# The order of the three partial products in a split-precision matmul group

## What is computed

```
def swiglu(x, w_gate, w_up, w_down):
    return (jax.nn.silu(x @ w_gate) * (x @ w_up)) @ w_down

h = h + 0.5 * swiglu(rmsnorm(h, ffn1_norm[l]), ffn1_w_gate[l], ffn1_w_up[l], ffn1_w_down[l])
proj = rmsnorm(h, mix_norm[l]) @ w_in[l]
```

## Time and profile before

| | |
|---|---|
| median of 3 runs | 2159.9 us (2159.9 to 2159.99) |
| the profiled execution, its time | 2160.47 us |
| the profiled execution, its span | 2158.5 us |
| mean granted TensorE clock | 1.0 |
| PE busy | 2152.0 us, 15592 matmuls |
| PEld busy | 2035.5 us, 15592 loads |
| DVE, ACT, POOL busy | 1560.7, 1221.6, 470.3 us |
| HBM read | 389.65 MB |

### The profile page before, as it was taken

One profiled execution on the slowest core, in us unless ns is written; L12 is line 12 of the kernel. 1 busy time (PEld: TensorE's weight loads), 2 busy tenths in 40 slices (PEclk: granted clock), 3 DMA queues, 4 the chain that ended last, 5 costly groups with the idle time before them and its releaser, 6 DMA issues.

```text
span 2158.5 us, 38713 instructions
## 1 busy us (share of the span) xinstructions
PE 2152.0 (100%) x15592; PEld 2035.5 (94%) x15592; DVE 1560.7 (72%) x2591; ACT 1221.6 (57%) x2047; POOL 470.3 (22%) x514
## 2 busy tenths in 40 slices
PE   9999999999999999999999999999999999999999
PEld 9999999999999999988988999889888999999888
DVE  8755977665765587876697586975876688887863
ACT  6544466444544456665566444654655677676652
POOL 1000532420340052231053000430321011101420
PEclk9999999999999999999999999999999999999999
DMA  8655435975785543565466554755565766664653
GB/s 279 222 162 183 144 118 159 237 185 177 193 209 182 171 157 111 183 209 187 160 207 205 189 186 144 233 189 191 187 195 176 210 200 172 178 195 142 227 177 104
DMA packets 424225, 395.81 MB, mean 183 GB/s; under 512 B 16864, under 2 KB 420448, under 8 KB 424048
## 3 DMA queue, kind: packets, MB, share of 16 engines
q1 hardware_dynamic: 410336, 375.22, 55.7%
q0 software_dynamic: 13424, 17.78, 4.0%
q10 hardware_dynamic: 288, 0.34, 0.0%
HBM read 389.65 MB, written 7.41 MB: 184 GB/s over the span
## 4 chain that ended last, share of the span: by engine, by line
PE 98%; DVE 1%; ACT 1%; DMA 0%; issue 0%; SPq 0%; ACTq 0%
PE ps L1755 30%; PE ps L1751 25%; PE ps L1753 17%; PE ps L1754 17%; PE ps L2097 1%; PE ps L2095 1%; PE ps L2096 1%; PE ps L1770 1%; PE ps L2063 0%; PE ps L2047 0%; PE ps L1873 0%; PE ps L2076 0%; PE ps L1918 0%; DVE t L1234 0%; PE ps L2030 0%; PE ps L2031 0%
## 5 line engine op out<-in xcount | busy, mean ns | idle before, releaser
L1755 PE MATMUL ps<-t 128*128 128x256 f32 (+1 forms) x5456 | 1547.4, 284 | 0.0
L1755 PEld LDWEIGHTS ps<-t 128*128 128x128 f32 x5456 | 1028.4, 188 | 0.1
L1234 DVE TENSOR_TENSOR t<-t 128x1024 fp32r<-128x1024 f32 (+1 forms) x722 | 875.7, 1230 | 162.2 <-ACT t L882 161.6
L1753 PE MATMUL ps<-t 128*128 128x272 f32 (+1 forms) x3036 | 875.7, 288 | 0.4 <-DVE t L1465 0.3
L1754 PE MATMUL ps<-t 128*128 128x272 f32 (+1 forms) x3036 | 865.3, 285 | 0.0
L882 ACT ACTIVATE t<-t 128x1024 fp32r<-128x1024 f32 (+1 forms) x722 | 728.3, 1030 | 229.2 <-PE ps L1755 223.6
L1751 PE MATMUL ps<-t 128*128 128x512 f32 x2420 | 840.2, 390 | 0.0
L1753 PEld LDWEIGHTS ps<-t 128*128 128x128 f32 x3036 | 570.8, 188 | 6.0 <-issue 3.3
L1754 PEld LDWEIGHTS ps<-t 128*128 128x128 f32 x3036 | 573.7, 189 | 0.9
L1751 PEld LDWEIGHTS ps<-t 128*128 128x128 f32 x2420 | 454.1, 188 | 95.0
L806 POOL TENSOR_TENSOR t<-t 128x256 f32<-128x256 f32 x110 | 100.6, 915 | 694.1 <-ACT t L1000 694.1
(11 more groups left out here) (208 smaller groups left out, 1583.8 us busy)
## 6 DMA issues: line engine op xcount, KB each, us to landing
t<-ffn_w_in SPq DMA_DIRECT2D x88, 1024.0 KB, 5.2
t<-ffn_w_gate SPq DMA_DIRECT2D x42, 1024.0 KB, 5.4
t<-ffn_w_up SPq DMA_DIRECT2D x42, 1024.0 KB, 7.4
t<-attn_w_qkv SPq DMA_DIRECT2D x72, 512.0 KB, 5.5
t<-ffn_w_down SPq DMA_DIRECT2D x32, 1024.0 KB, 5.2
t<-ffn_w_out SPq DMA_DIRECT2D x32, 1024.0 KB, 5.2
t<-w_in SPq DMA_DIRECT2D x28, 1024.0 KB, 5.0
t<-ffn_w_down SPq DMA_DIRECT2D x16, 768.0 KB, 4.4
```

Source lines behind the costliest of these rows:

```text
L1234: dve.tensor_tensor(wlo[:, plan.place[n], 0:nk, :], kept(u)[:, 0:nk, half * P:half * P + P], f32(whi[:, plan.place[n], 0:nk, :]), ALU.subt ...
L1753: pe.matmul(o, hi, xhi, start=i == 0, stop=False)
L1755: ins = pe.matmul(o, lo, xhi, start=False, stop=i == r.nk - 1)
```

## The change

In each group the product with the low weights comes first, then high weights by the high operand, then high weights by the low operand. In the joined form the 256-column product comes ahead of the 512-column one, except in the first turn of a tile: there the 512-column product stays first, because it starts the accumulation in both halves of the bank. The `start` and `stop` flags and the semaphore increment go to the products that are now first and last.

```diff
+                    end = i == r.nk - 1
                     if both is not None:
-                        pe.matmul(ps[:, r.banks[j], :].rearrange("p (m n) -> p m n", m=2), hi, both(k), start=i == 0, stop=False)
+                        whole = ps[:, r.banks[j], :].rearrange("p (m n) -> p m n", m=2)
+                        if i == 0:
+                            pe.matmul(whole, hi, both(k), start=True, stop=False)
+                            ins = pe.matmul(o, lo, xhi, start=False, stop=False)
+                        else:
+                            pe.matmul(o, lo, xhi, start=False, stop=False)
+                            ins = pe.matmul(whole, hi, both(k), start=False, stop=end)
                     else:
-                        pe.matmul(o, hi, xhi, start=i == 0, stop=False)
-                        pe.matmul(o, hi, xlo, start=False, stop=False)
-                    ins = pe.matmul(o, lo, xhi, start=False, stop=i == r.nk - 1)
+                        pe.matmul(o, lo, xhi, start=i == 0, stop=False)
+                        pe.matmul(o, hi, xhi, start=False, stop=False)
+                        ins = pe.matmul(o, hi, xlo, start=False, stop=end)
```

## The result

The changed kernel takes 2164.36 us (median of 14 runs, 2163.99 to 2164.59) against 2159.90 us (14 runs, 2159.41 to 2160.38). The ratio is 1.0021, 95% interval [1.0014, 1.0028]: 4.5 us slower. The forecast was 2160.8 us with a range up to 2162.7 us. The sign came out as forecast, the size did not: 4.5 us in place of 0.9. The profiled execution took 2164.49 us, with a span of 2162.6 us (2160.47 and 2158.5 before).

A forecast was written before the change was run, and what follows sets the result against it. PE's own steps were taken as the bound. Split form, weight loads, waits and releases at 0 plus seams at +0.9 us, on the median 2159.9 us, gave 2160.8 us, range 2158.2 to 2162.7 us.

The forecast's parts named there:

- The sign: Whole kernel: slightly slower, +0.9 us on the median, +0.04%, which a measurement would show as no change.
- The bound: PE is busy for the whole span at full clock; the changed lines' steps make about 1952 of 2158.5 us.
- Split form, 0 us: 3036 groups of three 256- or 272-column products: same cycle entered one place earlier, equal widths, so 0 us.
- Rival 2: Split form: neighbours sharing the high operand get cheaper, 34 us faster, 2126 us; chance 0.03.
- Weight loads, waits and releases, 0 us: Around the changed products: repeated weights, PE's waits and the banks' release times stay as before, 0 us.
- Rival 1: Joined form: a weight load is not ready behind two narrow products, 0.07 us at 220 places, +15.4 us; chance 0.03.
- The count of the seams, 215: Joined form: places where wide follows wide between tiles, 43 in each of five FFN stages.
- The price of a seam: Joined tile ends: wide-wide plus narrow-narrow against a pair, -0.005 to +0.010 us, taken as +0.004, times 215 = +0.9 us.
- The warning at the end: The three steps might depend on product order in a way the trace never showed; 0.2% of 1952 us is 4.3 us.
- Rival 3: Joined seams: wide behind wide costs much more because the second opens a new bank; 4.3 us need 0.02 each; chance 0.02.
- The rule of the Trainium skill: Joined seams: matmuls spaced by columns over clock plus a small constant, so a seam's four terms cancel to 0 us.

The follow-up runs named there:

- the rotated kernel: Kernel before, but in one-tile joined runs later turns go narrow, wide and the first turn's narrow product moves to the tile's end: 2160.05 us against 2160.08.
- the turned turn inside a tile: Kernel before, but in the joined form only row block 4's turn has its narrow product first: 2164.53 us against 2160.08, ratio 1.0020.
- the swapped weights: Kernel before, but high and low weights change places in row block 4's joined turn, widths still alternating: 2159.79 us against 2159.81, ratio 1.0000.

## Why the prediction was wrong, point by point

- **The bound** was right. PE's own steps set the time; waits and clock didn't change, and the 4.5 us are all steps of PE.
- **Split form, 0 us.** Right: 2160.32 against 2160.08 with this half alone. Rival 2 is out with it, there and in the unchanged 0.117 of the rows.
- **Weight loads, waits and releases, 0 us.** Right, by the loads' equal count and busy time, by the waits, and by the rotated kernel, which releases tiles from a narrow product as before and has the other narrow products ahead, at no cost. Rival 1 (a load bare behind two narrow products, 0.19 in the step) didn't happen: 0.12 from 890.47 to 890.59 and 0.11 from there on.
- **The count of the seams, 215,** was right: 215 x 0.020 is the loss within 0.2 us.
- **The price of a seam** is the step that failed: "+0.004 x 215 = +0.9 us", with the bound of +0.010. A seam cost 0.020. The value was not read off a wrong row. The sum took the seam for two steps, wide to wide and narrow to narrow, in place of one pair, and put every other step of the tile at no change. Those two steps measured 228.4 and 118.2 ns against a pair of 346.7, a difference of 0. So the term that was priced is 0, and that the forecast had the right sign comes from the choice of +0.004 between two rounded rows. The whole loss is in what was put at nothing without a reason: the step behind the second wide product (+6.7 ns) and those behind the next three (+16 ns, less about 3 ns at narrow ones). The trace of before has the effect, at a place that I hadn't read: I took the joined form's step from its middle, where it is settled, and not from the beginning of a joined stage. Timeline of PE there, kernel before:

```profile
873.26 0.40 PE L1751 MATMUL ps<-t 128*128 128x512 f32 x1
...
874.31 0.39 PE L1751 MATMUL ps<-t 128*128 128x512 f32 x1
```

  The first wide product behind a stretch of 256-column ones is recorded 0.40 long, and the first three pairs take 1.05 us, 0.350 each instead of 0.347. By the nanoseconds the three wide products have 234, 230 and 233 to the next start, and from the fourth on 228.
- **The warning at the end** ("the three steps depend on the order of the products in a way that this trace never showed") named what happened, and I gave it no chance and no width. The range ended 1.7 us short for this.
- **Rival 3** named one of the places where the steps are slow, and with "0.02 us a seam" the size. Its mechanism, a new bank behind a wide product, fell to the turned turn inside a tile.
- The rule of the Trainium skill beside the sum ("TensorE: Matmul & The Clock Gate", section "Back-to-back issue gap": spacing by columns plus a constant, given there for matmuls without weight loads between them) gave 0 us, further off. This trace disagrees with it: the spacing behind 512 columns varies from 0.228 to 0.235 us with the products before. The measurement decides.

Shown: the cost comes from breaks in the alternation of the widths (the swapped weights and the rotated kernel), arises at tile ends or inside alike, outlasts the break by some turns, and does not add up with the number of breaks. Not settled: what in PE remembers. Two regular sequences, wide-narrow and wide-narrow-narrow-wide, run at 0.347 us a pair. Sequences that repeat only after four or eight pairs ran at 0.349 or 0.350, and one of them at both. No experiment here looks inside that.

None of the versions beats the kernel before. Those with narrow first that come out level with it are the rotated one and the one with alternate turns in one-tile runs.

## What to carry to other kernels

Where PE is the bound for the whole span, a reordering that changes no count, width or wait can still move the time, since a product's step can depend on several products before it. Compare whole tiles (first start to first start, over many tiles), not only the neighbours at the place that is edited. Give a seam that occurs hundreds of times a price range as wide as the spread of the step anywhere in the trace, for each of several products behind it and not only for those at the seam. If products of two widths must be reordered, keep a short cycle of widths that runs on across tile ends; moving one product to the end of the tile was enough here.

## What the hardware showed that I had not expected

By the starts in the trace's nanoseconds, a product of 512 columns took 0.228 us to the next start in settled alternation and up to 0.235 us (recorded length 398 in place of 390 ns) for some turns after a break. The effect repeats from tile to tile to the nanosecond. Means over 30 one-tile runs, in us a tile: 2.7733 before, 2.7933 with one or with three turns turned round, 2.8000 with two of every four (2.7933 in one stage), 2.9000 with a narrow product more and 3.0200 with a wide one more. All differences from before, 0.0200, 0.0267, 0.1267 and 0.2467, are whole multiples of 0.00667 us (3, 4, 19 and 37 times), which is 16 cycles at 2.4 GHz, the level that the granted clock of 1.0 stands for. So a loss seems to come in whole units of that size for a whole tile, while its single steps move by less. That is read from these sums; no run tests it. A cycle that has wide behind wide and narrow behind narrow in every four products is as cheap as plain alternation.
